# Second block of a two-block transformer kernel: gate steps moved, the first token tile's softmax in halves, the gate's second product in two parts

## The reference, cut to what matters

```python
y_a = _rwkv7_time_mix(...) @ w_out_rwkv        # 8 heads of 64; its own gate: (y + bonus) * (sigmoid(p_g) @ w_gate_up)
y_b = _mla(...) @ w_out_mla                    # 8 heads, keys of 96, values of 64
merged = jax.nn.sigmoid(gate_a) * y_a + jax.nn.sigmoid(gate_b) * y_b
return merged @ w_out
```

```python
s = jnp.where(key_pos[None, :] <= q_pos[:, None], s, NEG_INF)
p = jax.nn.softmax(s, axis=-1)
return jnp.einsum('bhqk,bkhd->bqhd', p, v)
```

## Time and profile before

| | us |
|---|---|
| median of three runs | 2267.76 |
| the profiled execution, its own time | 2271.71 |
| its span, first to last instruction | 2269.9 |
| PE busy | 2040.7 (90%) |
| DVE busy | 894.1 (39%) |
| ACT busy | 718.2 (32%) |
| mean granted TensorE clock | 0.93 of full speed |

### The profile page before, as it was taken

The page is one execution under the profiler, slowest core; times in us unless marked ns, Lnnn a source line. Parts: engine busy times, 40 slices in busy tenths (PEclk is TensorE's granted clock), DMA queues, the critical chain, the costliest instruction groups (busy, mean ns, idle before and its releaser), DMA issues.

```text
span 2269.9 us, 38396 instructions
## 1 busy us (share of the span) xinstructions
PE 2040.7 (90%) x17052; PEld 1394.6 (61%) x17052; DVE 894.1 (39%) x1272; ACT 718.2 (32%) x1015; POOL 40.7 (2%) x65
## 2 busy tenths in 40 slices
PE   7999987888879999987788789989999999889998
PEld 6887433333328886433333248665899886758996
DVE  6444211110116444110101138446677474466774
ACT  5444111111115453111111135313444453144443
POOL 1000000000001000000000000000000000000000
PEclk9999788887889998888888889999999999999999
DMA  8236899999996257999999994022754350227540
GB/s 322 88 142 276 364 427 429 429 428 428 428 419 224 75 186 307 415 427 429 429 427 429 429 403 169 4 105 83 243 186 158 130 202 4 85 103 224 186 177 19
DMA packets 139667, 592.33 MB, mean 261 GB/s; under 512 B 5744, under 2 KB 59200, under 8 KB 114448
## 3 DMA queue, kind: packets, MB, share of 16 engines
q1 hardware_dynamic: 138432, 586.67, 65.1%
q0 software_dynamic: 1104, 3.70, 0.4%
HBM read 589.30 MB, written 1.05 MB: 260 GB/s over the span
## 4 chain that ended last, share of the span: by engine, by line
PE 69%; DMA 24%; DVE 3%; issue 2%; ACT 1%; SPq 1%; DVEq 0%; POOLq 0%; ACTq 0%; POOL 0%
PE ps L578 36%; DMA ring<-in_w_up 23%; PE ps L1182 11%; PE ps L2191 3%; PE ps L904 2%; PE ps L2006 2%; PE ps L1205 1%; PE ps L2238 1%; PE ps L1144 1%; DMA ring<-in_w_in 1%; PE ps L1214 1%; PE ps L595 1%; PE ps L1003 1%; PE ps L1099 1%; PE ps L1079 1%
## 5 line engine op out<-in xcount | busy, mean ns | idle before, releaser
L1182 PE MATMUL ps<-ring,area 128*32 128x512 f32 x1920 | 307.8, 715 | 120.9 <-DMA ring<-in_w_up 120.9
L554 DVE TENSOR_TENSOR ring_lo<-ring,slab_hi 128x2048 fp32r<-128x2048 f32 x136 | 311.3, 2292 | 225.2 <-ACT slab_hi L549 224.9
L549 ACT ACTIVATE slab_hi<-ring 128x2048 fp32r<-128x2048 f32 x136 | 260.0, 1913 | 285.0 <-PE ps L578 265.6
L1182 PEld LDWEIGHTS ps<-ring,area 128*32 128x32 f32 x1920 | 72.7, 128 | 311.4 <-issue 159.3
L578 PE MATMUL ps<-hT_hi,slab_hi 128*128 128x256 f32 x832 | 235.1, 283 | 3.0 <-DVE hT_lo L571 1.5
L578 PE MATMUL ps<-hT_lo,slab_hi 128*128 128x256 f32 x832 | 233.9, 281 | 0.0
L578 PE MATMUL ps<-hT_hi,ring_lo 128*128 128x256 f32 x832 | 232.8, 280 | 0.0
L1771 DVE TENSOR_TENSOR area<-ps,par 128x256 f32<-128x256 f32 x32 | 13.6, 425 | 477.2 <-PE ps L1144 477.2
L1205 PE MATMUL ps<-ring,area 128*32 128x512 f32 x992 | 161.9, 811 | 30.9 <-DVE area L1791 29.8
L1421 ACT ACTIVATE area<-ps 128x512 f32<-128x512 f32 x32 | 19.1, 597 | 536.1 <-PE ps L1182 536.1
L578 PEld LDWEIGHTS ps<-hT_hi,slab_hi 128*128 128x128 f32 x832 | 156.4, 188 | 4.3 <-issue 2.2
(11 more groups left out here) (384 smaller groups left out, 3165.2 us busy)
## 6 DMA issues: line engine op xcount, KB each, us to landing
ring<-in_w_up SPq DMA_DIRECT2D x62, 2048.0 KB, 20.3
ring<-in_w_down SPq DMA_DIRECT2D x62, 2048.0 KB, 21.6
ring<-in_w_gate SPq DMA_DIRECT2D x56, 2048.0 KB, 15.2
ring<-in_w_ffn_up SPq DMA_DIRECT2D x44, 1024.0 KB, 7.7
ring<-in_w_in SPq DMA_DIRECT2D x18, 2048.0 KB, 10.2
ring<-in_w_ffn_down SPq DMA_DIRECT2D x10, 2048.0 KB, 8.0
ring<-in_xattn_w_kv SPq DMA_DIRECT2D x8, 2048.0 KB, 16.6
area<-in_w_gate SPq DMA_DIRECT2D x6, 2048.0 KB, 14.0
```

The costliest lines, as they stand in the source:

```text
L549: return m.nc.scalar.activation(hi, whole, ACT.Copy)
L554: return m.nc.vector.tensor_tensor(lo, whole, hi, ALU.subtract)
L1182: ins = mm(ps[32 * g:32 * g + CAP, 1, :], m.tokT[:, k, :], gate_up[i][:, k % 4, (g % 2) * BANK:(g % 2 + 1) * BANK], start=k == 0, stop=k = ...
```

## The change

Three edits, all in the second block's mixer, so they act twice, once in each of its layers.

1. `GATE_FILLS`: the steps at `masks` go from 4 to 2, `second_wide` 2 to 3, `fourth` 2 to 3, `cross` 3 to 2, `close` 2 to 3, `rows` 3 to 5, `wu` 4 to 3. All later points keep their number; `rest` falls from 2 steps to 1.
2. `mla_parts()` gives four parts: tile 0's heads 0 to 3 and 4 to 7, then tile 1's as before. The signals `s2_full`, `s2_max` and `p2_rows` come four times. DVE's order becomes maximum 0, maximum 1, normalise 0, maximum 2, normalise 1, maximum 3, copy, normalise 2, normalise 3.
3. PE issues the time mix's gate product in two parts, each between the transposes of a tile and its output product. The output of tile 1 goes to bank 3 (before: bank 1), the gate product to banks 1 and 2.

```diff
-group("gqa_pe_scores", first=[("sc_full", 2)], second=[("s2_full", 3)])
+group("gqa_pe_scores", first=[("sc_full", 2)], second=[("s2_full", 4)])
...
-    for point, n in (("open", 8), ("prep", 5), ("sums", 3), ("masks", 4), ("second", 3), ("second_wide", 2), ("fourth", 2),
-                     ("whole", 2), ("fourth_wide", 3), ("eighth", 2), ("keys", 4), ("block", 3), ("block_wide", 2), ("cross", 3),
-                     ("close", 2), ("rows", 3), ("wu", 4), ("q", 2), ("g", 1), ("h", 4)):
+    for point, n in (("open", 8), ("prep", 5), ("sums", 3), ("masks", 2), ("second", 3), ("second_wide", 3), ("fourth", 3),
+                     ("whole", 2), ("fourth_wide", 3), ("eighth", 2), ("keys", 4), ("block", 3), ("block_wide", 2), ("cross", 2),
+                     ("close", 3), ("rows", 5), ("wu", 3), ("q", 2), ("g", 1), ("h", 4)):
...
-            if h == MH - 1 or t and h == MH // 2 - 1:
+            if h in (MH // 2 - 1, MH - 1):
                 ins.then_inc(s("s2_full"), 1)
 
-    done = 0
+    pe.wait_ge(*at("gateup_in", l))
+    up = m.par2("gate_up")
+
+    def gate_up(b):
+
+        for i in range(2):
+            tile = 2 * b + i
+            ins = mm(half_bank(m, GATE_UP_BANKS[b], i), up[:, tile * P:(tile + 1) * P], m.gg, start=True, stop=True)
+        ins.then_inc(s("gateup_full"), 1)
+
     for t in range(NT):
...
-            if j == 0 or t and j == 2:
-                pe.wait_ge(*at("p2_rows", l, t + j // 2 + 1))
+            if t == 0 or j % 2 == 0:
+                pe.wait_ge(*at("p2_rows", l, 2 * t + j // (t + 1) + 1))
...
+        gate_up(t)
         pe.wait_ge(*at("p2_cols_a", l, (1, 3)[t]))
         pe.wait_ge(*at("p2_cols_d", l, (1, 3)[t]))
...
-                ins = mm(ps[r:r + HD, t, (h // 2) * P:(h // 2 + 1) * P], m.vm[:, kt, h * HD:(h + 1) * HD], m.pmT[:, h, kt, :],
+                ins = mm(ps[r:r + HD, O2_BANKS[t], (h // 2) * P:(h // 2 + 1) * P], m.vm[:, kt, h * HD:(h + 1) * HD], m.pmT[:, h, kt, :],
...
-    pe.wait_ge(*at("gateup_in", l))
-    up = m.par2("gate_up")
-    for b in range(2):
-        for i in range(2):
-            tile = 2 * b + i
-            ins = mm(half_bank(m, 2 + b, i), up[:, tile * P:(tile + 1) * P], m.gg, start=True, stop=True)
-        ins.then_inc(s("gateup_full"), 1)
+O2_BANKS = (0, 3)
+GATE_UP_BANKS = (1, 2)
...
-    return ((0, 0, MH), (1, 0, MH // 2), (1, MH // 2, MH))
+    return tuple((t, h, h + MH // 2) for t in range(NT) for h in (0, MH // 2))
...
-        if i == 2:
+        if i == 3:
             act.wait_ge(*at("p2_T", l, 1))
...
     maximum(1)
     normalise(0)
     maximum(2)
+    normalise(1)
+    maximum(3)
     dve.wait_ge(*at("p2_T", l, 2))
     mla_prob_columns(m, v.tensor_copy, 0, 1).then_inc(s("p2_cols_d"), 1)
-    normalise(1)
     normalise(2)
+    normalise(3)
```

More of the change, by code:

```diff
@@ L298 @@
 group("gqa_act_cols", first=[("pT_a", 4)], second=[("p2_cols_a", 3)])
-group("gqa_dve_max", first=[("sc_max", 2)], second=[("s2_max", 3)])
+group("gqa_dve_max", first=[("sc_max", 2)], second=[("s2_max", 4)])
 group("gqa_dve_cols", first=[("pT_d", 4)], second=[("p2_cols_d", 3)])
-group("mla_dve_rows", second=[("p2_rows", 3)])
+group("mla_dve_rows", second=[("p2_rows", 4)])
 group("gqa_dve_out", first=[("at_rows", 2)], second=[("o2_cols", 2)])
@@ L3173, in vector_rwkv_out @@
         dve.wait_ge(*at("gateup_full", l, b + 1))
-        tt(m.yaT[:, 2 * b:2 * b + 2, :], m.y[:, 2 * b:2 * b + 2, :], two(ps[:, 2 + b, :]), ALU.mult).then_inc(s("ya_cols"), 1)
+        tt(m.yaT[:, 2 * b:2 * b + 2, :], m.y[:, 2 * b:2 * b + 2, :], two(ps[:, GATE_UP_BANKS[b], :]), ALU.mult).then_inc(s("ya_cols"), 1)
 def vector_mla(m, dve, l):
@@ L3242, in vector_mla @@
         dve.wait_ge(*at("o2_full", l, t + 1))
-        v.tensor_copy(m.o2T[:, :, t * P:(t + 1) * P], ps[:, t, :].rearrange("p (i b) -> p i b", b=P)).then_inc(s("o2_cols"), 1)
+        v.tensor_copy(m.o2T[:, :, t * P:(t + 1) * P], ps[:, O2_BANKS[t], :].rearrange("p (i b) -> p i b", b=P)).then_inc(s("o2_cols"), 1)
 def scalar_end(m, act):
```

## The result

The changed kernel took 2257.85 us (median of 4 runs, 2257.41 to 2259.0); the kernel before, beside it, 2269.84 (2267.06 to 2273.89). The ratio is 0.9942, with a 95% interval of 0.9925 to 0.9959: faster by 0.4 to 0.75%, or 9 to 17 us. The forecast was 2258.5 us and 9.3 us less. The profiled execution after took 2257.99 us, its span is 2256.2; before 2269.9. Of that difference of 13.7 us, what lies ahead of the first gate step gives -2.5 (that step came at 1407.01 and not 1404.48; over the fourteen traces of this case it comes between 1401.3 and 1408.4), the stretch from there to the second layer's L2006 gives 16.5, and what follows -0.2.

The account below looks back on a forecast made before the run. It took PE, busy 90% of the span, as the bound, with instruction-fetch holes and softmax waits in the mixer. Gate moves 3.9 plus softmax 5.4 make 9.3 us: 2267.8 - 9.3 = 2258.5 us, range 2255.5 to 2261.5.

Parts of the forecast that it names:

- What bounds it, and that the gain reaches the end: Outside the second block's mixer PE runs products unbroken, so whatever the mixer gives up reaches the end, once per layer.
- Now six records of gate steps come first ... the hole shrinks from 3.96 to 2.7 us: Rows 3 to 5, wu 4 to 3: hole behind L2314 shrinks by 1.3 us, about as much in the second layer.
- After 'fourth' all stands as before ... Worth 0: Moves at masks, second_wide, fourth: first layer's 0.52 and 2.42 us holes stay, worth 0; second layer gains 0.6 us.
- Clock, 0.2 us a layer: Behind the L2314 hole: shorter PE idle time may spare the lower clock; 0.2 us a layer taken from 0 to 4.4.
- Softmax, 2.7 us a layer: Scores to L2006: earlier last normalise 0.95 us, shorter copies 0.8, split gate product 0.95; 5.4 us in all.
- The sum: Both layers' mixers: gate moves 3.9 us plus softmax 5.4 make 9.3 us.
- rival D: After L2314: shorter idle times spare the lower clock in both layers, 4.0 us more, 2254.5 us; chance 0.12.
- B: Gate stretch: issue holes are PE's queue time for small instructions, not fetching; moves keep every hole, 2262.4 us; chance 0.13.
- C: Softmax: the halves bring nothing because tile 1's scores set the pace; 5.8 us left, 2262.0 us; chance 0.17.
- E: Score products: the lower clock falls on them in both layers, making it slower, 2272.5 us; chance 0.06.
- The signs named ahead: Profile: L2314 hole 2.2 to 2.8 us, second layer's 0.59 gone, 2.42 kept, first exp 2.5, L2006 17.7, copy wait 0.8.
- one sign of being wrong: Wrong if L2314's hole keeps 3.5 us, PE's clock is 0.5 in new places, or L2006 starts over 19 us after scores.

Follow-up runs that it names:

- masks_only: Kernel before with only masks 4 to 2, second_wide 2 to 3 and fourth 2 to 3; 2264.33 us, ratio 0.9959.
- softmax_only: Kernel after with the gate steps of before, so softmax halves and split gate product alone; 2265.32 us, ratio 0.9970.
- gateup_only: Kernel before with the gate product in two parts alone, tile 0's softmax whole; 2269.08 us, ratio 0.9987.
- late_release: Kernel after with the slot for the w_out slab load released five gate steps later, behind the u products; 2252.06 us, ratio 0.9914.
- halves_only: Kernel before with tile 0's softmax in halves alone, the gate product whole at the end; 2265.96 us, ratio 0.9971.
- after_again: The kernel after, unchanged, run once more with a profile of its own; 2258.46 us, ratio 0.9929 to the kernel before.
- late_mid: late_release with two gate steps, one from wu and one from q, put halfway into the h products (L2345); 2248.55 us, ratio 0.9905.
- balanced: late_release with four steps a layer moved: rows 5 to 3, g 1 to 3, keys 4 to 3, eighth 2 to 3; 2251.84 us, ratio 0.9903.

## Why the prediction was right, and where it was not

The time came out 0.65 us from the forecast, and faster as forecast. The softmax part is right in its mechanism and nearly in size; the gate part has the wrong size, because one term put at 0 and 0.6 us is worth some 3 us a layer.

- **What bounds it, and that the gain reaches the end**: held. The 302.4 us between the layers did not change.
- **"Now six records of gate steps come first ... the hole shrinks from 3.96 to 2.7 us"**: 2.62 in the first layer, 1.86 in the second for the 2.2 forecast.
- **"After 'fourth' all stands as before ... Worth 0"**: this step failed. I held the block's floor of 4 us against the edges as PE executes them, found 3.9 us in each block, and stopped. The packet is asked for by PE's sequencer, which runs ahead of the products where the block is already there (0.6 us ahead of them after, 1.1 us behind them before, as read above); that it could not be ahead before because each packet was late from the 5.6 us block on is my reading of the two rows of packets. masks_only measures this term as 3.3 and 3.2 us up to L2314 (3.3 to 4.4 and 1.7 to 3.2 against all traces with the old numbers), for 0 and 0.6 forecast, and in the first layer it contains the stretch at the lower clock behind the 2.42 us hole (1.4 us), which I did not even list. My list of holes was short as well: it left out 0.36 and 1.61 us in the first layer and 1.84, 0.73, 0.74, 0.49 and 1.58 in the second, and it is around the 1.84 that the second layer gained (3.2 us of holes to 1.0).
- **Clock, 0.2 us a layer**: mis-sized. In the first layer the low stretch behind L2314 halved (0.50 from 1484.0 to 1490.7 before, from 1483.8 to 1487.1 after); from L2314 to L2325 it took 8.45 us, for 11.37 before; of these 2.9 us the hole is 1.3, the step that was moved away 0.7, and the clock some 1.2 for the 0.2 forecast. In the second layer it kept its length, and behind L2345 a stretch at the lower clock came up that the trace of before has not:
```profile
1954.90:1958.10 3.20, 3.20 (x9) 2.42 (x9) 2.29 (x4) 0.69 (x1) 0.00 (x0) 0.50 0.00 0
```
In the first layer such a stretch stood there before, too, and softmax_only and gateup_only have it in both layers, so the gate moves did not bring it.
- **Softmax, 2.7 us a layer**: 3.1 and 3.2 by the chain. The terms were 1.35 (0.95 forecast), 0.6 (0.8) and 1.0 (0.95) with L2006's start in the timeline, from which I had worked; the chain has 1.15 for the last. The maximum over 512 columns took the 0.69 us that I took for it. That PE would wait 0.8 us for DVE's copy ahead of L2006 is there as 0.78.
- **The sum**: gates 10.1 us for 3.9, softmax 6.3 for 5.4. The forecast time is met partly by luck. The stages gave 16.5 us in the profiled executions, whose spans differ by 13.7 and the medians by 12.0; and the median of before moved from 2267.76 to 2269.84 with one more run. A gain of 12 us for 9.3 lies nearer to rival D in size, though not for D's reason alone.
- **Rivals**: B falls with masks_only and late_release. C falls with halves_only. E is not what the kernel does as a rule, but its mechanism exists: the clock did fall on the score products, in one layer of some executions, at 5.0 us.
- **The signs named ahead**: the hole behind L2314 (2.62), the first exp (2.5 us), L2006 (17.4 for 17.7) and the wait for the last copy (0.78) came as said or close to it. The 2.42 us hole did not stay, the second layer's 0.59 did not go altogether (0.56 is left at 1891.24), and one sign of being wrong is there, PE's clock at 0.5 where the trace of before has it not, the one above.

## What to carry to other kernels

Where PE runs hundreds of small products, count its instructions in blocks of 256 and ask of each block how long it executes; one that is shorter than the fetch of the next (3.4 to 4.1 us here) leaves a hole, and one that is longer leaves the fetching idle, so move long products from the long blocks into the short ones, and inside them, not into the stage ahead. Keep large loads from starting while a short block runs: one semaphore moved by five gate steps took 2.1 to 4.3 us a layer off the stretch behind it, about as much as the softmax edit took off its own. And sum such a pipeline by its requests, not by the times at which the instructions execute.

## What the runs showed of the hardware that I had not expected

- An instruction packet that meets the 2 MB slab load starts 3.1 to 4.3 us behind the block's edge and not about 1 (1482.5 for an edge at 1479.0); the hole in L2314 went when the load began later.
- Holes of this kind cost twice: PE's idle 2 to 4 us are followed by a stretch at the lower level of 1.2 GHz in most cases (not, for example, behind the 2.04 and 2.12 us of after_again), in which 12 gate products take 4.0 to 5.5 us and not 2.8 to 3.0. With holes under 1.2 us everywhere the mixers of late_mid had none in the profiled execution.
- The clock can stay at 1.2 GHz for 13.6 us with PE busy in all of them (balanced, above).
